# Moving the sums of a layer's down weights from its up products to the input projection, in slices

## The reference, cut to what matters

```python
def _sq_relu_mlp(x, w1, w2):
    return jnp.square(jax.nn.relu(x @ w1)) @ w2

def _attn_project(h, w_in):
    n, t, _ = h.shape
    z = h @ w_in
    qa, qb, ka, va, kb, vb = jnp.split(...)
```

## Time and profile before

| | us |
|---|---|
| median of 3 runs | 2173.14 (2172.93 to 2173.84) |
| the profiled execution | 2173.05 |
| its span in the trace | 2171.2 |
| PE busy | 2118.4 (98% of the span) |
| DVE busy | 1026.0 (47%) |
| ACT busy | 818.7 (38%) |
| POOL busy | 133.8 (6%) |
| DMA queue of SP, share of 16 engines | 51.6% |

### The profile page before, as it was taken

The page is one execution under the profiler, slowest core; times in us unless marked ns, Lnnn a source line. Parts: engine busy times, 40 slices in busy tenths (PEclk is TensorE's granted clock), DMA queues, the critical chain, the costliest instruction groups (busy, mean ns, idle before and its releaser), DMA issues.

```text
span 2171.2 us, 31832 instructions
## 1 busy us (share of the span) xinstructions
PE 2118.4 (98%) x13227; PEld 1912.4 (88%) x13227; DVE 1026.0 (47%) x1503; ACT 818.7 (38%) x1507; POOL 133.8 (6%) x214
## 2 busy tenths in 40 slices
PE   7999999999999999999999999999999999999998
PEld 7999877777789999999888878789999999888886
DVE  5120287566553333333645467663333335444475
ACT  5111397545332223232523245452222224333343
POOL 1000131000110000000000013220000000000011
PEclk9999999999999999999999999999999999999999
DMA  5331301098426666665876553436666566665464
GB/s 172 87 86 36 141 26 34 19 406 329 141 80 225 219 225 217 220 212 217 283 246 228 170 163 98 144 128 229 228 216 226 212 219 235 240 224 169 161 216 137
DMA packets 205963, 394.21 MB, mean 182 GB/s; under 512 B 18749, under 2 KB 100853, under 8 KB 197500
## 3 DMA queue, kind: packets, MB, share of 16 engines
q1 hardware_dynamic: 199628, 387.45, 51.6%
q10 hardware_dynamic: 6192, 4.72, 0.7%
HBM read 273.12 MB, written 119.24 MB: 181 GB/s over the span
## 4 chain that ended last, share of the span: by engine, by line
PE 76%; DVE 2%; ACT 1%; issue 1%; POOL 0%; DMA 0%; POOLq 0%; DVEq 0%; SPq 0%; ACTq 0%
PE ps L1914 34%; PE ps L1953 27%; PE ps L3097 4%; PE ps L1971 3%; PE ps L1413 2%; PE ps L1923 1%; PE ps L3017 1%; PE ps L1434 1%; PE ps L1474 1%; PE ps L2990 1%; PE ps L1455 0%; DMA t_b_raw<-scratch_t_ops 0%; PE ps L3117 0%; PE ps L3030 0%; POOL stats L1529 0%
## 5 line engine op out<-in xcount | busy, mean ns | idle before, releaser
L1953 PE MATMUL ps<-t_b_hi,t_a_hi 128*128 128x512 f32 x896 | 351.7, 393 | 2.1 <-DVE t_y L1823 1.1
L1953 PE MATMUL ps<-t_b_lo,t_a_hi 128*128 128x512 f32 x896 | 348.9, 389 | 0.0
L1953 PE MATMUL ps<-t_b_hi,t_a_lo 128*128 128x512 f32 x896 | 348.9, 389 | 0.0
L1914 PE MATMUL ps<-m_xT_hi,t_w_lo 128*128 128x384 f32 (+1 forms) x1480 | 326.7, 328 | 0.0
L1914 PE MATMUL ps<-m_xT_lo,t_w_hi 128*128 128x384 f32 (+1 forms) x1480 | 326.7, 328 | 0.0
L1914 PE MATMUL ps<-m_xT_hi,t_w_hi 128*128 128x384 f32 (+1 forms) x1480 | 326.7, 328 | 0.0
L1680 DVE TENSOR_TENSOR t_w_lo<-t_raw,t_w_hi 128x1024 fp32r<-128x1024 f32 x64 | 78.3, 1225 | 427.0 <-ACT t_w_hi L1676 427.0
L1744 DVE TENSOR_TENSOR t_a_lo<-t_a_raw,t_a_hi 128x1024 fp32r<-128x1024 f32 x112 | 137.2, 1225 | 300.3 <-ACT t_a_hi L1737 300.3
L1737 ACT ACTIVATE t_a_hi<-t_a_raw 128x1024 fp32r<-128x1024 f32 x112 | 118.8, 1061 | 396.3 <-PE ps L1971 275.8
L1676 ACT ACTIVATE t_w_hi<-t_raw 128x1024 fp32r<-128x1024 f32 x64 | 67.7, 1058 | 504.9 <-PE ps L1914 492.2
L1914 PEld LDWEIGHTS ps<-m_xT_hi,t_w_lo 128*128 128x128 f32 x1480 | 252.9, 188 | 0.0
(11 more groups left out here) (284 smaller groups left out, 3010.2 us busy)
## 6 DMA issues: line engine op xcount, KB each, us to landing
scratch_t_ops<-t_t SPq DMA_DIRECT2D x32, 1280.0 KB, 5.5
scratch_s_ops<-t_s SPq DMA_DIRECT2D x32, 1280.0 KB, 4.5
t_a_raw<-scratch_s_ops SPq DMA_DIRECT2D x80, 512.0 KB, 3.9
t_b_raw<-scratch_t_ops SPq DMA_DIRECT2D x80, 512.0 KB, 4.7
t_raw<-mlp_w SPq DMA_DIRECT2D x64, 512.0 KB, 4.1
t_w_raw<-mlp_w SPq DMA_DIRECT2D x32, 1024.0 KB, 7.7
scratch_a_ops<-t_h SPq DMA_DIRECT2D x32, 512.0 KB, 5.5
t_a_raw<-scratch_a_ops SPq DMA_DIRECT2D x32, 512.0 KB, 3.4
```

Source lines behind the costliest of these rows:

```text
L1914: mm = self.nc.tensor.matmul(out, a[:, k, :], b_[:, k, c], start=(k == 0 and x == 0), stop=(k == KT - 1 and x == 2))
L1953: mm = self.nc.tensor.matmul(self.core.ps[:, self.BANK[idx] + tp, :], a[s][:, kk, tp * P:(tp + 1) * P], w[s][:, kk, :], start=(c == 0 and ...
```

## The change

For layer 0 alone, the sums are no longer made beside the up products (`Mlp(..., sums_here=False)`). A new class `DownSums` makes them during the input projection, in 64 units: 16 pairs times four slices of 128 columns. A unit is two loads by SP into one of three raw buffers, four DVE instructions into one of two result buffers, and one store by SP. All its DRAM pieces are 128 columns, 512 bytes. Layer 1 is left as it was.

```diff
+class DownSums:
+    SLICES = D // 2 // P
+    COUNT = PAIRS * SLICES
...
+    def load(self, sp, j):
+        if j >= self.COUNT:
+            return
+        if j >= 3:
+            sp.wait_ge(self.ready, j - 2)
+        i, x = divmod(j, self.SLICES)
+        for e in range(2):
+            src = self.pairs[i][:, e, :].rearrange("p (h n) -> p h n", h=2)[:, :, x * P:(x + 1) * P]
+            sp.dma_start(self.raw[:, j % 3, e], src).then_inc(self.raw_in[j % 3], 16)
+
+    def store(self, sp, j):
+        i, x = divmod(j, self.SLICES)
+        sp.wait_ge(self.ready, j + 1)
+        sp.dma_start(self.t_ops[i][:, :, x * P:(x + 1) * P], self.t[:, j % 2]).then_inc(self.stored[j % 2], 16)
+
+    def move(self, sp, first, last):
+        for j in range(first, last):
+            self.store(sp, j)
+            self.load(sp, j + 3)
...
+    def combine(self, dve, count):
+        nc = self.core.nc
+        for j in range(self.done, self.done + count):
+            w, t = self.raw[:, j % 3], self.t[:, j % 2]
+            dve.wait_ge(self.raw_in[j % 3], 32 * (j // 3 + 1))
+            if j >= 2:
+                dve.wait_ge(self.stored[j % 2], 16 * (j // 2))
+            b11, b12, b21, b22 = w[:, 0, 0], w[:, 0, 1], w[:, 1, 0], w[:, 1, 1]
+            nc.vector.tensor_tensor(t[:, 0:2], w[:, :, 0], w[:, :, 1], ALU.add)
+            nc.vector.tensor_tensor(t[:, 2], b11, b22, ALU.add)
+            nc.vector.tensor_tensor(t[:, 3], b12, b22, ALU.subtract)
+            nc.vector.tensor_tensor(t[:, 4], b21, b11, ALU.subtract).then_inc(self.ready, 1)
+        self.done += count
...
             if n == 2:
                 for t in range(xs, NT):
                     load_x(t)
+                for j in range(3):
+                    down.load(sp, j)
+            if n == 3:
+                down.move(sp, 0, 3)
+            elif n == 4:
+                down.move(sp, 3, 5)
+            elif n == 5:
+                down.move(sp, 5, 16)
+            elif n == 7:
+                down.move(sp, 16, 28)
+            elif n == 8:
+                down.move(sp, 28, 40)
             if n >= 2:
                 sp.wait_ge(lo_done, n - 1)
...
+        down.move(sp, 40, down.COUNT)
...
             if m == Q + KT // 2:
                 act.wait_ge(v_stored, 64)
+                down.wait_stored(act)
...
                 tn.take_lo(nc, dve, i + 1)
             if i == NT - 2:
                 lo(1)
-        for n in range(2, NV + 2):
-            lo(n)
+            if i >= 4:
+                down.combine(dve, 1)
+        lo(2)
+        down.combine(dve, 11)
+        lo(3)
         for m in range(Q):
             for n in turns_of(m):
                 take_rows(n)
             if m % 2 == 0:
                 lo(NV + m // 2 + 2)
+            down.combine(dve, 6)
+        down.combine(dve, 12)
         for n in range(NV + 2 + Q // 2, len(chunks)):
             lo(n)
...
     def up_loads(self, sp):
-        for i in range(2):
-            self.load_w2(sp, i)
+        if self.sums_here:
+            for i in range(2):
+                self.load_w2(sp, i)
...
-                self.store_t(sp, n // 2)
-                if n // 2 + 2 < PAIRS:
-                    self.load_w2(sp, n // 2 + 2)
+                if self.sums_here:
+                    self.store_t(sp, n // 2)
...
-                if n % 2 == 0:
-                    m0.combine_t(dve, n // 2)
-                else:
+                if n % 2 == 1:
                     m0.combine_s(dve, n // 2)
```

More of the change, by code:

```diff
@@ L291 @@
     VA_T = ROWS + 2 * NT * P * 4
+    DOWN_RAW = VA_T + TOK * 4
+    DOWN_T = DOWN_RAW + 3 * 4 * P * 4
+    DOWN_END = DOWN_T + 2 * 5 * P * 4
 class Attend:
@@ L356, with __init__, wait_stored @@
     columns: int
-def in_project(core, identity, x_src, gain, w_in, xT_hi, xT_lo, qT, kaT, kbT, v, outs):
+class DownSums:
+    SLICES = D // 2 // P
+    COUNT = PAIRS * SLICES
+    def __init__(self, core, w2, t_ops):
+        self.core, self.t_ops = core, t_ops
+        self.pairs = w2.rearrange("(e f p) n -> f p e n", e=2, p=P)
+        self.raw = core.at("in_down_raw", core.base + In.DOWN_RAW, [P, 3, 2, 2, P])
+        self.t = core.at("in_down_t", core.base + In.DOWN_T, [P, 2, 5, P])
+        self.raw_in = [core.sem(f"in_down_raw_in{s}") for s in range(3)]
+        self.ready = core.sem("in_down_ready")
+        self.stored = [core.sem(f"in_down_stored{s}") for s in range(2)]
+        self.done = 0
+    def load(self, sp, j):
[15 more added lines that the diff above has]
+            self.load(sp, j + 3)
+    def wait_stored(self, eng):
+        for s in range(2):
+            eng.wait_ge(self.stored[s], 16 * self.COUNT // 2)
+    def combine(self, dve, count):
[11 more added lines that the diff above has]
+        self.done += count
@@ L364, in in_project @@
+def in_project(core, down, identity, x_src, gain, w_in, xT_hi, xT_lo, qT, kaT, kbT, v, outs):
     nc = core.nc
@@ L1576, with __init__ @@
     SETS = (0, 768, 512)
-    def __init__(self, core, tag, w1, w2, ops, sb, xT_hi, xT_lo):
+    def __init__(self, core, tag, w1, w2, ops, sb, xT_hi, xT_lo, sums_here):
+        self.sums_here = sums_here
         self.core, self.nc = core, core.nc
@@ L1591, in __init__ @@
         self.s_ready = core.sem(tag + "s_ready")
-        self.t_ready = core.sem(tag + "t_ready")
         self.s_stored = [core.sem(f"{tag}s_stored{s}") for s in range(2)]
-        self.t_stored = [core.sem(f"{tag}t_stored{s}") for s in range(2)]
+        if sums_here:
+            self.t_ready = core.sem(tag + "t_ready")
+            self.t_stored = [core.sem(f"{tag}t_stored{s}") for s in range(2)]
         self.operand_in = [core.sem(f"{tag}operand_in{s}") for s in range(2)]
@@ L1636, in load_operands @@
                 sp.wait_ge(self.s_stored[s], 32 * (c + 1))
-                sp.wait_ge(self.t_stored[s], 16 * (c + 1))
+                if self.sums_here:
+                    sp.wait_ge(self.t_stored[s], 16 * (c + 1))
         if g >= 2:
@@ L1661, in up_loads @@
             if n % 2 == 0:
-                self.store_t(sp, n // 2)
-                if n // 2 + 2 < PAIRS:
-                    self.load_w2(sp, n // 2 + 2)
+                if self.sums_here:
+                    self.store_t(sp, n // 2)
+                    if n // 2 + 2 < PAIRS:
+                        self.load_w2(sp, n // 2 + 2)
             elif n < 2 * PAIRS - 1:
@@ L1726, in split_operands_hi @@
     def split_operands_hi(self, act, g):
-        act.wait_ge(self.operand_in[g % 2], 16 * (PAIRS // 2) + 32 * (g // 2 + 1))
+        act.wait_ge(self.operand_in[g % 2], (16 * (PAIRS // 2) if self.sums_here else 0) + 32 * (g // 2 + 1))
         if g == 1:
@@ L2108, in trunk @@
     zn = [zn_early, zn_mid, zn_early, zn_mid, zn_early, zn_mid, zn_late[:, 0, :], zn_late[:, 1, :], zn_mid]
-    m0 = Mlp(core, "m0_", ins["mlp_w1"][0], ins["mlp_w2"][0], operands[0], sb, xT_hi, xT_lo)
-    m1 = Mlp(core, "m1_", ins["mlp_w1"][1], ins["mlp_w2"][1], operands[1], sb, xT_hi, xT_lo)
+    m0 = Mlp(core, "m0_", ins["mlp_w1"][0], ins["mlp_w2"][0], operands[0], sb, xT_hi, xT_lo, False)
+    m1 = Mlp(core, "m1_", ins["mlp_w1"][1], ins["mlp_w2"][1], operands[1], sb, xT_hi, xT_lo, True)
     core.shifted, core.roots = core.sem("ms_shifted"), 0
@@ L3193, in build @@
             qT_offset = nc.sbuf_top
+            assert core.base + In.DOWN_END <= qT_offset
             assert core.base + Attend.SINK + 64 + 2 * PT * NH * 4 <= qT_offset
@@ L3205, in build @@
             q_a = core.at("sa_q_a", core.base + Sample.Q_A, [P, NB, NH * NQ])
-            inp = in_project(core, tables["identity"], (xp, xs), gains[0], ins["attn_w_in"], a_xT_hi, a_xT_lo, qT,
+            down = DownSums(core, ins["mlp_w2"][0], operands[0]["t_ops"])
+            inp = in_project(core, down, tables["identity"], (xp, xs), gains[0], ins["attn_w_in"], a_xT_hi, a_xT_lo, qT,
                              kaT, kbT, v, outs)
```

## The result

The changed kernel takes 2220.67 us (median of 4 runs, 2219.76 to 2222.94) against 2173.03 (2172.23 to 2173.84) for the one before on the same chip: a ratio of 1.022, with a 95% interval of 1.0204 to 1.0236. That is 47.6 us more where 36.0 were forecast, inside the range and slower, as forecast, but above the likeliest band (2203 to 2216). The span of its profiled execution is 2218.9 us.

What follows compares the result with a forecast made beforehand. The prediction took PE, busy 98% of the span, as the bound. Stalls of 11.0, 9.7 and 9.7, clock 5.1 and block 10's 0.5 made 36.0 us on 2173.05: 2209 us, range 2188 to 2228.

Steps and rivals of the forecast that it cites:

- What bounds the kernel: Whole kernel: PE, busy for 98% of the span, so an edit helps only where PE waits or its matmuls are slowed.
- what is removed: 0: Layer 0's up products: taking the sums, loads and stores away gains 0 us, as PE runs there without a break.
- Where PE stands: Input projection: PE waits at its third turn in blocks 2, 4 and 6, about 10 us each, nearly nothing in 3 and 5.
- The V phase: First five units between the norms of x: costed at 0, up to 1 us if the first load lands late.
- The group of six: Six units behind `lo` in the projection last 13.3 us; waits of 11.0 us in block 2, 9.7 in blocks 4 and 6.
- The 18 units and block 10: After m = 5, 18 units and `lo(7)`, units behind the first six at 2.1 us; PE waits 0.5 us.
- rival (c): Projection units: loads and stores disturb each other, landing a microsecond later each; 2.3 us a unit, total 2220, chance 0.13.
- about 1: DMA share forecast from 107 us to the end of the sums in the projection.
- 512-byte rule: DMA pieces: the skill's claim that 512 bytes reach line rate; forecast read about 274 GB/s against it, 318 for 1-KB pieces.
- rival (a): Unit transfers: small pieces cost no more than large ones, 1.67 us a unit; total 2202.5, chance 0.15.
- The chunk in front: Behind `lo`, SP issues the next weight chunk first; it keeps the DMA engines 3.36 us, ahead of the group's first store.
- The clock: Behind each of three stalls in blocks 2, 4 and 6, PE runs at a lower clock: 3 x 1.7 = 5.1 us.

Runs made afterwards that it cites:

- e2: All loads, stores and sums of `DownSums` left out of the changed kernel, layer 0's down product reading plain blocks of `w2`; 2172.16 us, ratio 1.0002 to the kernel before.
- e9: Changed kernel with `lo(7)` ahead of the last twelve units instead of behind them; 2209.94 us, ratio 1.0171 to the kernel before.
- e3: Changed kernel with DVE's sums kept in place, but no stores and only the first three loads; 2180.88 us, ratio 1.0042 to the kernel before.
- e10: Changed kernel with units spread, few before urgent takes and low parts, the rest in the Q blocks, ACT's store wait later; 2171.44 us, ratio 0.9996.
- e6: Changed kernel with six raw and four result buffers in place of three and two; 2197.66 us, ratio 1.011 to the kernel before.
- e4: Changed kernel with three of each unit's four sums left out from the third unit on, all DMAs kept; 2209.91 us, ratio 1.0168 to the kernel before.
- e5: Changed kernel with 32 units of 256 columns (1-KB pieces), two raw and two result buffers of double size; 2200.33 us, ratio 1.013 to the kernel before.
- e8: Changed kernel with SP issuing the next weight chunk behind four of the group's unit moves; 2226.69 us, ratio 1.0247 to the kernel before.
- e1: Changed kernel with the six units made before `lo` after even m, SP's moves shifted to match; 2199.96 us, ratio 1.0129 to the kernel before.

## Why the prediction was right, and where its sizes were off

**What bounds the kernel; what is removed: 0.** Right. The up run is 372.00 us as before and e2 is 1.0002. That 12.00 us belongs to the block and not to its neighbours shows again in the changed kernel's windows (columns as in the earlier trace rows): an up block, now without the sums.

```profile
707.20:719.20 12.00, 12.00 (x74) 12.00 (x73) 1.23 (x1) 3.43 (x8) 0.00 (x0) 1.00 0.20 57
```

DVE is busy for 1.23 us and not 4.26, the DMA share is 0.20 and not 0.98, and the 74 matmuls take the same 12.00 us.

**Where PE stands.** Right: at the third turn, in blocks 2, 4 and 6, 0.2 to 0.5 us in 3 and 5 (0.0 and 0.1 us longer in e9), and in block 10 for `lo(7)`. The V phase cost nothing that can be told from chance (0.25 us; 0 to 1 forecast). The eleven units behind it ended at 90.3 us and not at about 80, 3.0 us a unit; that was a miss too, but `lo(3)` behind them still ended at 92.5, in time for block 2 at 102.08, so it cost nothing. e3 and e10 bear the mechanism out from both sides.

**The group of six.** Forecast 13.3 us behind `lo`, 14.65 in block 2; measured 14.3, 14.4 and 15.6 (107.32 to 122.91). Waits 11.8, 10.4 and 10.6 in place of 11.0, 9.7, 9.7: 2.4 us too little in all (1.7 by the repeat in e9, whose three waits are 11.5 and 20.6 us).

**The 18 units and block 10: the mis-sized term.** Here the sum went by 2.1 us a unit, the time of the DMA engines, and gave 38.1 us and a loss of 0.5. Measured were 43.8 us, 2.43 a unit, and a loss of 6.6. This is the largest miss, 6.1 of some 11 us. The step that failed is the store's way, counted as 1.2 + 1.17 + 0.2 = 2.6 us for a store that has the engines to itself. With that a round of two units is 1.0 + 2.6 us, 1.8 us a unit, less than the engines' 2.1, and so the forecast took the engines for the bound. From the changed kernel by tile: first the stores, then the loads.

```profile
L393 SPq DMA_DIRECT2D scratch_t_ops<-in_down_t x64: 513/563/1537, 37.5 to 245.9; - x64
...
DMA to landing us min/median/max: 2.8/3.7/9.4
```

```profile
L387 SPq DMA_DIRECT2D in_down_raw<-mlp_w x128: 539/647/2171, 32.2 to 240.8; - x128
```

A store lands 3.7 us after its issue in the median, and 3.5 (2.8 to 4.9) within the 18 units. With two result buffers a unit may begin when the store of two units before has landed, so two units take one round: 0.96 of DVE (e3: 5.74 / 6), 3.5 to land, and 0.4 left over, 4.86 us or 2.43 each. Part of what is left over is SP, which is occupied for 35.9 of the 43.8 us: a unit was done at 210.22, and its store was issued at 211.31, behind two loads. This round is what rival (c) had worked out, "(1.02 + 3.6) for two", with landings a microsecond later. Its chance, 0.13, was too low against 0.58 for the landing that only quiet rows had shown. That its total, 2220 us, is what came is in part luck: it had the groups 2 to 3 us longer and the 18 units 3.5, and they were 1 us and 5.7 us longer; and that loads and stores disturb each other, its reason, no run shows.

That the round and not the engines' capacity set the pace is shown by e6: its stores land no sooner (medians 3.9 and 4.4), but with more of them in flight a unit takes 2.07 us, near the DMA-bound figure of the forecast, at a DMA share of 0.99. (SP is occupied for 33.4 of those 37.3 us, so it is not far from being the bound itself.) The changed kernel's own DMA share says it too. Windows of the changed kernel over the 18 units:

```profile
200.00:225.00 25.00, 23.59 (x128) 23.62 (x129) 11.33 (x43) 4.21 (x7) 0.00 (x0) 0.87 0.89 248
225.00:247.00 22.00, 18.02 (x109) 17.73 (x107) 10.38 (x37) 4.20 (x7) 0.00 (x0) 1.00 0.84 232
```

The forecast had "about 1". One thing fits the round only in part: e4 takes some 0.7 us of DVE off each unit and should by it gain 0.35 a unit, but gained 0.23. What takes its place isn't separated: over e4's 18 units the DMA share is 0.97 and SP is occupied for 35.3 of 39.6 us. Why a landing is slower under load (issues, both directions, memory) was not separated either.

The Trainium skill, DMA: Bandwidth & Descriptors, Latency and other measured facts, gives a wide spread for the memory's latency, 0.2 us on average and 2 us at high load, and makes it the main part of a DMA's fixed cost. The spread of the landings here, 2.8 to 9.4 us for stores of one size, goes the same way, but part of it is queueing, and no run here tells the two apart. As to the 512-byte rule that the forecast weighed: e6, with 512-byte pieces, got a unit through in 2.07 us and e5, with 1-KB pieces, in 1.99, and e5 was waiting for its loads. Over the 18 units e6 moved 280 GB/s at a share of 0.99 and e5 297 at 0.94, so 283 against 316 GB/s at full share, near the 274 and 318 that the forecast read from the earlier trace rows. This fits a price for small pieces, but e5 has half as many DMAs as well, and the two weren't separated; rival (a)'s 1.67 us a unit was reached by neither. (In that rival's working, two of DVE's 1.02 and a round of 2.3 make 4.3 and not 4.1 us; nothing hangs on it.)

**The chunk in front.** The forecast charged the chunk's 3.36 us to the group. Its length bears most of that out (e8's groups are 2 to 3 us shorter), but not that the time could be won: e8 lost 6 us by it. A term of a sum isn't a saving when the thing has to pass somewhere.

**The clock: 5.1 forecast, at most 7.7 measured.** Beyond PE's waits the blocks are 8.1 us longer (46.72 less 38.66, the table's two sums). 2.2, 1.5 and 2.5 of it in the three blocks are near the 1.7 assumed; 1.5 are block 10's, whose stall was forecast too short to have any. The 0.3 in blocks 3 and 5 are not the clock's, which stayed at 1.00 there: a stop costs 0.16 to 0.17 us more than its wait even so, which the forecast left out. Windows in block 2 of the changed kernel:

```profile
113.00:114.00 1.00, 0.00 (x0) 0.00 (x0) 0.00 (x0) 0.00 (x0) 0.00 (x0) 1.00 1.24 280
114.00:115.00 1.00, 0.00 (x0) 0.00 (x0) 0.00 (x0) 0.00 (x0) 0.00 (x0) 0.72 1.12 309
115.00:116.00 1.00, 0.00 (x0) 0.00 (x0) 0.74 (x3) 0.00 (x0) 0.00 (x0) 0.50 1.15 345
...
124.00:126.00 2.00, 2.00 (x8) 2.00 (x8) 1.45 (x6) 0.00 (x0) 0.00 (x0) 0.50 0.96 273
...
128.00:130.00 2.00, 2.00 (x13) 2.00 (x12) 0.00 (x0) 0.97 (x3) 0.00 (x0) 0.98 0.83 230
```

PE stops at 111.9 and is at 0.50 (1.2 GHz) from 115 on. It resumes at 123.7 and does 8 matmuls in two microseconds where it later does 13; near 128 it is back at 2.4 GHz.

**The sum.** Waits 2.4 short, the odd blocks 1.1, the time beyond the waits in blocks 2, 4 and 6 1.1, block 10 6.1, the V phase 0.25: 11.0 us, which with the 36.0 forecast is the 47.0 at the end of block 13. At the start of the up run the difference is 45.8, mostly because 24 matmuls before it ran 1.5 us faster (last section), and the span's is 47.7; the 1.9 us that come in between weren't followed.

## What to carry to other kernels

Before work goes into an in-order engine's list, write down for each wait of the bound engine what stands ahead of its release, and price that by the round trip of the transfers through its buffers under load, not by the engine's own time: here 6 us of DVE's time were 14 us of its list. Moving work out from under an engine that is busy without a gap gains nothing, whatever it frees on the other engines. If such work has to move, it goes behind the last thing that the bound engine is waiting for; deeper buffers shorten the loss (47 to 25 us), placement removes it.

## What the runs showed that I had not expected

**The same gap costs clock in one trace and not in another.** I took 1.7 us a stall from the gap ahead of the last third of up block 0. Chains, the kernel before, then the changed one:

```profile
655.93 5.32 PE ps L1923 x24
```

```profile
703.29 3.78 PE ps L2009 x24
```

In both PE has waited for DVE for 2.37 us just before, and the same 24 matmuls follow: 5.32 us, for most of them at a granted clock of 0.57 to 0.58, or 3.78 us with the clock at 1.00. All thirteen traces of this case have this wait of 2.4 us; in eleven the 24 matmuls last 5.29 to 5.33 us, in two (the changed kernel, e1) 3.78 and 3.79. Likewise e3's three waits of 1.9 us: blocks 2 and 4 grew by 3.6, with the clock down to 0.50 and 0.54 in windows of 2 us, and block 6 by 2.1, with the clock at 1.00. In these traces a short gap's price beyond the wait is one of two values, some 1.5 to 1.7 us or next to nothing, and the length of the gap doesn't say which.

**SP's share of a DMA is not small.** With the queue loaded, SP is occupied for 0.56 us by a store and 0.65 by each load (medians), so a unit of three costs it 1.9 us, nearly as much as the 2.10 that the forecast gave the 16 engines for its data.
